# Gate/up bias: from matmuls into PSUM to a broadcast load and an addition on VectorE

## What is computed

```python
gu = jnp.matmul(hx, wgu) + bgu                        # (288, 2048), gate and up interleaved
gate = jnp.minimum(gu[:, 0::2], SWIGLU_LIMIT)
up = jnp.clip(gu[:, 1::2], -SWIGLU_LIMIT, SWIGLU_LIMIT)
act = gate * jax.nn.sigmoid(SWIGLU_ALPHA * gate) * (up + 1.0)
y = jnp.matmul(act, wdn) + bdn
return acc + c[:, None] * y.astype(jnp.float32), None
```

## Time and profile before

| | us |
|---|---|
| median of 3 runs (lowest, highest) | 1361.01 (1356.37, 1366.43) |
| span of the profiled execution | 1365.9 |
| PE busy | 1291.0 (95%) |
| DVE busy | 291.9 (21%) |
| ACT busy | 168.8 (12%) |
| mean DMA rate | 333 GB/s |

### The profile page before, as it was taken

How to read it: one execution, slowest core, us unless ns; L and a number is a source line. 1 busy time by engine, 2 the same in 40 slices (tenths; PEclk the granted TensorE clock), 3 DMA queues, 4 the chain that set the end, 5 groups by cost and what they waited for, 6 DMA issues and landing times.

```text
span 1365.9 us, 15103 instructions
## 1 busy us (share of the span) xinstructions
PE 1291.0 (95%) x5845; PEld 571.0 (42%) x5846; DVE 291.9 (21%) x674; ACT 168.8 (12%) x428; POOL 45.2 (3%) x75
## 2 busy tenths in 40 slices
PE   7999877889999999999999999999999999999993
PEld 5777642352434334343434242424343433434330
DVE  1034543421120303030202111111112030303025
ACT  0124431210101000010101010101010100001002
POOL 0111100200000000000000000000000000000002
PEclk9999897958999999999999999999999999999997
DMA  7961767445899989899998989898989898989830
GB/s 269 343 219 64 249 239 304 156 173 220 366 427 397 423 361 427 352 409 371 370 409 369 412 368 410 369 413 367 411 369 411 358 418 356 427 353 412 365 128 36
DMA packets 79813, 454.25 MB, mean 333 GB/s; under 512 B 6746, under 2 KB 19042, under 8 KB 30242
## 3 DMA queue, kind: packets, MB, share of 16 engines
q1 hardware_dynamic: 77456, 440.17, 79.2%
q0 software_dynamic: 1728, 10.75, 2.1%
q10 hardware_dynamic: 594, 2.86, 0.5%
HBM read 450.22 MB, written 11.93 MB: 338 GB/s over the span
## 4 chain that ended last, share of the span: by engine, by line
PE 91%; DVE 3%; DMA 2%; ACT 2%; issue 1%; POOL 0%; SPq 0%; POOLq 0%; DVEq 0%; ACTq 0%
PE bank L849 35%; PE bank L891 17%; PE bank L825 10%; PE bank L602 7%; PE bank L905 7%; PE bank L836 5%; PE bank L568 3%; PE bank L740 3%; PE bank L690 1%; PE bank L667 1%; ACT actT L953 1%; ACT xg L953 1%; DMA out<-kstage 1%; DMA kring<-in_state_k_win 1%; PE bank L615 0%
## 5 line engine op out<-in xcount | busy, mean ns | idle before, releaser
L849 PE MATMUL bank<-ring,xg 128*64 128x512 f32 x2032 | 479.8, 633 | 0.0
L849 PEld LDWEIGHTS bank<-ring,xg 128*64 128x64 f32 x2032 | 150.6, 146 | 336.8 <-issue 336.8
L891 PE MATMUL bank<-ring,actT 128*64 128x512 f32 x1024 | 225.4, 598 | 3.8 <-ACT actT L953 3.8
L1386 DVE TENSOR_TENSOR acc<-acc,bank 128x512 f32<-128x512 f32 (+1 forms) x96 | 65.6, 683 | 584.0 <-PE bank L905 584.0
L825 PE MATMUL bank<-pick,hx 128*128 128x128 f32 (+1 forms) x768 | 142.7, 318 | 1.1 <-DVE pick L1352 1.1
L891 PEld LDWEIGHTS bank<-ring,actT 128*64 128x64 f32 x1024 | 79.8, 138 | 138.6 <-issue 135.8
L825 PEld LDWEIGHTS bank<-pick,hx 128*128 128x128 f32 (+1 forms) x768 | 109.0, 195 | 43.9 <-issue 15.5
L1074 ACT ACTIVATE sig<-gate 128x256 f32<-128x256 f32 x64 | 26.6, 416 | 624.0 <-DVE gate L1368 624.0
L602 PE MATMUL bank<-xT,wblk 128*128 128x288 f32 x384 | 99.4, 417 | 0.5 <-DVE xT L1134 0.5
L905 PE MATMUL bank<-ybuf,spread 128*128 128x512 f32 (+1 forms) x192 | 91.6, 612 | 1.2 <-ACT ybuf L953 1.2
L602 PEld LDWEIGHTS bank<-xT,wblk 128*128 128x128 f32 x384 | 73.5, 195 | 20.4 <-DVE xT L1134 0.7
(11 more groups left out here) (159 smaller groups left out, 608.5 us busy)
## 6 DMA issues: line engine op xcount, KB each, us to landing
ring<-in_w_gate_up SPq DMA_DIRECT2D x127, 2048.0 KB, 10.4
ring<-in_w_down SPq DMA_DIRECT2D x64, 2048.0 KB, 10.4
wblk<-in_w_in SPq DMA_DIRECT2D x12, 1024.0 KB, 8.0
kring<-in_cache_k_moba SPq DMA_DIRECT2D x16, 256.0 KB, 4.3
out<-in_state_k_win POOLq DMA_DIRECT2D x8, 512.0 KB, 5.9
out<-in_state_v_win POOLq DMA_DIRECT2D x8, 512.0 KB, 5.6
vring<-in_cache_v_moba SPq DMA_DIRECT2D x16, 256.0 KB, 6.5
wout<-in_w_out SPq DMA_DIRECT2D x4, 1024.0 KB, 8.1
```

Of the source, the lines that this page charges most:

```text
L849: ins = nc.tensor.matmul(bank[n][64 * e:64 * e + 64, :], xg[:, k, 64 * e:64 * e + 64], w[:, 2048 * e + 512 * n:2048 * e + 512 * n + 512], ...
L891: ins = nc.tensor.matmul(bank[4 + half][64 * e:64 * e + 64, :], actT[:, j, 64 * e:64 * e + 64], w[:, at:at + 512], start=(j == 0), stop=(j ...
L1386: V.tensor_tensor(acc[0:n, t, c], acc[0:n, t, c], bank[4 + half][0:n, :], ALU.add).then_inc(S.added, 1)
```

## The change

The bias matmuls and their weights in `keep` go. A buffer `bias` of 128 x 2048 numbers (1 MB) takes the pair's two rows, each broadcast over its expert's 64 partitions by one DMA of 512 KB. It lies where `xT` lies in the attention part, so `load_bias(0)` moves behind the wait for the router's last product. DVE adds the bias when it takes the sums from PSUM, one addition each for gate and up, and clips afterwards from SBUF. The buffer is free when the eight additions of a pair are done (`biased`), and SP waits for that before it issues the next pair's bias. The first weight matmul of each bank now starts the sum.

```diff
 C_SEL = C_IOTA + CHUNKS * SLOTS
-C_HEAD = C_SEL + 8 * SLOTS
+C_HEAD = C_SEL
...
-    bias_rows = place("bias_rows", [8, 512])
...
+    bias = place("bias", [128, 2 * D], at=x_at)
...
         def load_bias(p):
-            src = b_gate_up[0, pair_of(p), :].rearrange("e (n c) -> (e n) c", c=512)
-            sp.dma_start(bias_rows[:, :], src).then_inc(S.bias_in, 16)
-
-        load_bias(0)
+            src = b_gate_up[0, pair_of(p), :]
+            for e in range(2):
+                sp.dma_start(bias[64 * e:64 * e + 64, :],
+                             src[e:e + 1, :].broadcast_to([64, 2 * D])).then_inc(S.bias_in, 16)
...
         sp.dma_start(ln_b[:, :], ln2_b[0:1, :].broadcast_to([128, D])).then_inc(S.ln2_in, 16)
+        sp.wait_ge(S.logitsT_done, 3)
+        load_bias(0)
...
         def next_bias(i):
-            sp.wait_ge(S.bias_used, i + 1)
+            sp.wait_ge(S.biased, i * 8 + 8)
             load_bias(i + 1)
...
             pe.wait_ge(S.act_ready, i * 4)
-            pe.wait_ge(S.bias_in, i * 16 + 16)
-            for n in range(4):
-                for e in range(2):
-                    ins = nc.tensor.matmul(bank[n][64 * e:64 * e + 64, :],
-                                           keep[0:8, C_SEL + SLOTS * (4 * e + n):C_SEL + SLOTS * (4 * e + n + 1)],
-                                           bias_rows[:, :], start=True, stop=False)
-            ins.then_inc(S.bias_used, 1)
...
-                                               start=False, stop=(k == KC - 1))
+                                               start=(k == 0), stop=(k == KC - 1))
...
             dve.wait_ge(S.act_turned, i * 2)
+            dve.wait_ge(S.bias_in, i * 32 + 32)
...
-                    V.tensor_scalar(gate[:, c], bank[n][:, 0:512:2], LIMIT, None, ALU.min).then_inc(S.clipped, 1)
-                    V.tensor_scalar(up[:, c], bank[n][:, 1:512:2], LIMIT, -LIMIT, ALU.min, ALU.max).then_inc(S.dve_moe, 1)
+                    b = slice(512 * n, 512 * n + 512, 2), slice(512 * n + 1, 512 * n + 512, 2)
+                    V.tensor_tensor(gate[:, c], bank[n][:, 0:512:2], bias[:, b[0]], ALU.add).then_inc(S.biased, 1)
+                    V.tensor_tensor(up[:, c], bank[n][:, 1:512:2], bias[:, b[1]], ALU.add).then_inc(S.biased, 1)
+                    dve.wait_ge(S.biased, i * 8 + (2 * n + 1))
+                    V.tensor_scalar(gate[:, c], gate[:, c], LIMIT, None, ALU.min).then_inc(S.clipped, 1)
+                    dve.wait_ge(S.biased, i * 8 + (2 * n + 2))
+                    V.tensor_scalar(up[:, c], up[:, c], LIMIT, -LIMIT, ALU.min, ALU.max).then_inc(S.dve_moe, 1)
```

More of the change, by code:

```diff
@@ L82, in constant_tables @@
     keep[:, C_IOTA:C_SEL] = np.arange(CHUNKS * SLOTS)
-    for r in range(8):
-        keep[r, C_SEL + r * SLOTS:C_SEL + (r + 1) * SLOTS] = 1
     keep[p, C_HEAD + p // DS % H] = 1
@@ L213, in build_layer @@
         weights_ready counted comb_turned combT_ready spread_down route_ready unit0 unit1 unit2 unit3 unit4
-        unit5 unit6 unit7 unit_used first_in att_in gn_in bias_in bias_used picked gathered xg_ready
+        unit5 unit6 unit7 unit_used first_in att_in gn_in bias_in biased picked gathered xg_ready
         gate_up_done clipped sigmoided act_ready act_turned actT_ready pickw_turned spread_ready down_done
@@ L474, in more @@
         def more(i, p, c, m, odd):
-            sp.wait_ge(S.bias_used, i)
+            sp.wait_ge(S.biased, i * 8)
             load_bias(p)
@@ L481, in none @@
         def none(i, m, odd):
-            sp.wait_ge(S.bias_used, i)
-            sp.sem_inc(S.bias_in, 16)
+            sp.wait_ge(S.biased, i * 8)
+            sp.sem_inc(S.bias_in, 32)
             for u in range(UNITS):
@@ L937, in none @@
         def none(i, m, odd):
-            for sem, n in ((S.gathered, 2), (S.bias_used, 1), (S.unit_used, UNITS - 2), (S.gate_up_done, 4),
+            for sem, n in ((S.gathered, 2), (S.unit_used, UNITS - 2), (S.gate_up_done, 4),
                            (S.pickw_turned, 1), (S.act_turned, 2), (S.down_done, 1), (S.mixed, 6)):
@@ L1424, in none @@
         def none(i, m, odd):
-            for sem, n in ((S.picked, 2), (S.clipped, 4), (S.dve_moe, 8), (S.act_ready, 4), (S.added, 6)):
+            for sem, n in ((S.picked, 2), (S.biased, 8), (S.clipped, 4), (S.dve_moe, 8), (S.act_ready, 4), (S.added, 6)):
                 skip(dve, sem, i, n, 6 if sem is S.added else 0)
```

## The result

| | before | after |
|---|---|---|
| median of the runs | 1358.72 us (1356.37 to 1366.43, 4 runs) | 1387.03 us (1373.96 to 1401.93, 4 runs) |
| span of the profiled execution | 1365.9 us | 1378.9 us (its own time 1380.73) |

The change makes the kernel slower: the ratio to before is 1.017, with a 95% interval of 1.0096 to 1.0244. The forecast was 1338 us, range 1303 to 1358, so the time is outside the range and on the other side of no change. The profiled execution shows a span of 1378.9 us where the sum said 1342.2, 36.7 us more.

A forecast was written before the change was run, and what follows sets the result against it. DMA was taken as the bound: 59.2 us of weights plus 4.7 us of bias load make 63.9 us a pair. Fifteen pairs from 347.0 plus the closing work gave 1342.2, less 4: 1338 us, range 1303 to 1358.

The forecast's parts named there:

- the price of the bias load: Each pair's two 64-partition bias loads: doubled transfer time, 4.93 us less 0.2 hidden, taken as 4.7 us; chance 0.53.
- the far bound: Highest price considered for a pair's bias load: broadcast with a straggling tail, 4.9 us, doubled for half partitions to 9.8 us.
- DMA becomes the bound: Per pair of experts, DMA would need 63.9 us against PE's 58.0, so PE waits 5.9 us.
- A unit is 4.93 us: Weight stream: one 2,048 KB unit takes 4.93 us at 425 GB/s, twelve make 59.2 us a pair.
- Matmuls removed, the slow clock behind them: Before gate/up on PE: dropping the bias matmuls saves their 3.58 us and 3.34 us of slow clock a pair.
- The add on VectorE: Eight additions a pair after gate/up: a quarter becomes 2.15 us, hidden in pairs 0 to 14, +2.7 us in the last.
- The moved wait: SP's next bias issue waits for VectorE's last addition: delays pair 0's restart to 344.6 from 336.8, costs nothing later.
- The rival at full rate: Bias load's two halves run side by side over all partitions: pairs of 61.7 us, kernel 1305 us; chance 0.17.
- The drag of a queue without rest: DMA queue, never idle, falls short of its bulk rate by 1 us a pair: kernel 1353 us; chance 0.20.
- The straggling broadcast: Bias load's broadcast source makes one DMA engine straggle each pair: 9.8 us instead of 4.7, kernel 1414 us; chance 0.08.
- The whole PE saving: All PE time saved by dropping the bias matmuls, 6.9 us a pair, comes through: kernel 1251 us; chance 0.02.
- The 4 us taken off for the profiled execution: End of the sum: profiled execution before lay 4.9 us above the runs' median, so 1342.2 was lowered to 1338.

The follow-up runs named there:

- drain: The changed kernel, but the next pair's bias is issued only when all weight units of the pair before have landed; 1387.03 us.
- noload: The changed kernel with only the first pair's bias loaded and used by all pairs, waits and additions kept; 1263.90 us, ratio 0.928.
- k128: The kernel before, its bias matmuls over 128 rows instead of 8, the added rows zero; 1312.13 us, ratio 0.962.
- twoq: The changed kernel with the second expert's bias half issued from ScalarE's queue, at the same time as SP issues the first; 1383.21 us.
- one128: The changed kernel with one 1 MB bias load, one row broadcast over all 128 partitions, instead of two of 512 KB; 1300.61 us, ratio 0.955.
- rows64: The changed kernel with the same two 64-partition loads, but each partition reads its own row of the gate/up weights; 1389.04 us.
- pieces: The changed kernel with each half load cut into four of 128 KB, the two partition halves taking turns; 1363.37 us, ratio 1.0007 to the kernel before.
- both128: The changed kernel with its two loads made into one over 128 partitions, whose source repeats each bias row 64 times; 1793.58 us, ratio 1.316.
- cols128: The changed kernel with two 512 KB loads, each over all 128 partitions and half of the columns; 1302.16 us, ratio 0.956.
- half: The changed kernel, but from the second pair on only the first expert's bias (512 KB, 64 partitions) is loaded; 1345.88 us.
- woven: The kernel before, bias matmuls over 128 rows (120 of them zero) and moved into the combine of the pair before; 1321.27 us.

## Why the prediction was wrong

**The step that failed is the price of the bias load**: 4.93 less 0.2, "4.7 us, near the x_sample row". The last gate/up (L829) ends at 1327.8 (1289.3 forecast) although everything began 4.9 us early. So fifteen pairs took 43.4 us more than summed, 2.9 each: 66.8 us a pair. Less 58.8 for twelve units the load costs 8.0 us on average, 7.0 to 10.0 from the third pair on. It is a term that was mis-sized, and its mechanism was named in part. The doubling is right where the load starts from rest (half rate for 5 us for pair 1's load, and for every load of drain). The rule of the Trainium skill that I weighed ("SBUF — State Buffer", "Door 1: The DMA port swizzle") holds there with 209 to 225 GB/s against 428. The rest of the price, some 3 us, is that the weights beside it are slowed as well. My rows could not show it: x_sample and b_down have 128 KB each, and both went by soon after a rest (x_sample is issued at 1.65 us, b_down at 216.98 behind two units, on a queue that was idle up to 217). I read their factors (1.5 and 1.8) as a doubling partly hidden. They bounded a load on its own; the average price in a saturated queue lay between the upper bound I kept for width (4.93) and the far bound (9.8), and I gave that space to a broadcast that costs nothing.

The prediction had the point at which this decides: no change at a load of 6.2 us, slower by 1% from 7.2. At 8.0 the outcome follows. The 0.08 for the slower side hung on the straggling source alone; a load whose price has no row should have had the sign-changing size spread over all its possible causes.

**Point by point.**
- *DMA becomes the bound*: right. Share 1.00, PE waits 85.6 us for units of gate/up, and a fall of the clock stays hidden. The clock did fall again, behind PE's own waits (0.95 over the long window; PE did nothing from 887 to 889, where it was 0.63, and resumed at 0.50, as the windows of 2 us from 887 on show); noload, where PE hardly waits, has 1.00.
- *A unit is 4.93 us*: 4.90 (58.8 for twelve), since the stream makes 428 GB/s and not 425. 6 us less in all.
- *Matmuls removed, the slow clock behind them*: right, by k128: it keeps them at 3.43 us and loses the fall.
- *The add on VectorE*: hidden, as said. A quarter takes 1.60 to 1.94 us (2.15 forecast), as additions follow each other at 0.34. In the last pair the down matmuls start at 1334.4, 6.6 us behind L829's end (8.0 forecast, 5.3 before): the add cost 1.3 us there and not 2.7.
- *The moved wait*: right at the start, wrong later. The restart came 3.8 us after gate/up's end (4.6 forecast), at 339.7 and not 344.6, since the attention part ended 4.1 us earlier than I took over. "DMA idle once, and not again" holds to about 930. Then part of the engines are idle before each bias issue (share 0.45 from 1066 to 1068), 0.2 to 1.2 us a pair as a mean of the 16. The sum had the engines in step, with one landing time for a unit; they were not. It is 4.7 us in all, so 0.3 of the 8.0 us are this and not the load.
- *The rival at full rate* (the halves side by side): false, by after and twoq. *The drag of a queue without rest*: false for loads of full width, by noload's 428 GB/s. *The straggling broadcast*: false, by one128 and rows64. *The whole PE saving*: false; even noload, at 1264, has DMA at 1.01.
- *The 4 us taken off for the profiled execution*: of no use. This time the median of the runs lies 6 us above it.

**What stays open.** Why the price climbs from 7 to 10 us over the pairs and falls back, the same in both profiles, is argued and not shown. Each half-width load in a full queue leaves the engines further apart, until the early ones run empty before the next issue and so lose their lead. The packet records fit this, and so does rows64: there no engine is idle before an issue from the second pair on, and its pairs go on rising, to 69.4 us in the last. pieces has no idle engine either, and wavers between 66.0 and 67.4 us, so this isn't the whole account. K (engines at different places hinder each other) explains that a half costs over twice its doubling, that a rest shortens the dip, and both128's slow units; it wasn't seen engine by engine. Open without an account are why packets take 342 ns in some stretches of drain, and why the kernels with half-width loads spread over 0.9 to 2.7% from run to run, and one128, cols128 and noload over 0.3 to 0.4%. The kernel before is no firm mark there: mostly it spreads over 0.5 to 0.7%, but beside half, drain, twoq and woven it gave 1333.46 and 1343.81 among five runs of 1361.81 to 1364.72.

## What to carry to other kernels

Where DMA is near its limit, bring everything into SBUF over all 128 partitions, or count a narrow load at several times its bytes (here 8.0 us for 2.45), since it slows its neighbours in the queue too. No run here brought two different rows to the two halves at full rate: one128 and cols128 leave part of the bias out, and both128, which doesn't, is the slowest of all. When a removed cost (here the clock fall behind matmuls of few rows) can be removed in place, try that before trading it against another engine: zero rows gave 3.8%, and the change, which moved the work, lost 1.7%.

## What the runs showed of the hardware

- Two loads of 64 partitions (1 MB in all) cost about 5 us from rest and 7 to 10 us in a full queue; one load of 128 partitions costs 2.45 us in the same place.
- The same load from a source with an outermost dimension of 2 left two engines alone at work behind all others, at 53 GB/s and a share of 0.13, and took the kernel to 1794 us.
- Behind a rest of 2 us before each half-width load, 122 to 149 packets a pair were slow (over 400 ns for 309), where the load has 128; without the rest up to 326 were.
- Weights streamed at 428 GB/s for 800 us, with a DMA share of 1.01.
- Sixteen matmuls of 8 rows were followed by a clock of 0.50; the same over 128 rows, 120 of them zero, kept it at 1.00.
